# Scan of a hybrid decoder step: one 128-column moving operand for the products on a and r

## What is computed

```python
def wkv7_step(S, inp):
    r, d, k, v, a, b = inp
    sa = jnp.einsum('bhij,bhj->bhi', S, a)
    S = S * d[:, :, None, :] + sa[..., None] * b[:, :, None, :] + v[..., None] * k[:, :, None, :]
    return S, jnp.einsum('bhij,bhj->bhi', S, r)
...
    S_new, o = lax.scan(wkv7_step, S0.astype(f32), seq)
```

## Time and profile before

| | |
|---|---|
| median of 3 runs | 2534.65 us (2529.38 to 2535.4) |
| profiled execution, its own time | 2534.88 us |
| its span in the trace | 2532.9 us |
| mean granted clock of TensorE | 0.967 |
| TensorE busy | 2401.2 us, 95% of the span |
| VectorE, ScalarE, GpSimd busy | 44%, 15%, 21% |
| the eight iterations of the scan | 1266.6 to 1486.1 us |

### The profile page before, as it was taken

How to read it: one execution, slowest core, us unless ns; L and a number is a source line. 1 busy time by engine, 2 the same in 40 slices (tenths; PEclk the granted TensorE clock), 3 DMA queues, 4 the chain that set the end, 5 groups by cost and what they waited for, 6 DMA issues and landing times. The chain is left out here.

```text
span 2532.9 us, 51980 instructions
## 1 busy us (share of the span) xinstructions
PE 2401.2 (95%) x22210; PEld 2277.4 (90%) x22210; DVE 1117.5 (44%) x2477; ACT 387.7 (15%) x879; POOL 526.4 (21%) x270
## 2 busy tenths in 40 slices
PE   5999999999999899999788889989999999999996
PEld 4999999999999899888377775979999999999995
DVE  4533434333344454343666663137333444443336
ACT  4100000000000223344611132031000000000003
POOL 3312122121121131111511034123211212212200
PEclk8999999999999999999799997989999999999997
DMA  9223221111111221011310012122111111111102
GB/s 328 84 100 100 69 80 50 50 50 33 50 28 38 87 79 55 26 34 39 117 25 5 5 32 86 42 100 84 51 33 50 28 38 50 50 50 50 33 0 79
DMA packets 160616, 151.19 MB, mean 60 GB/s; under 512 B 21472, under 2 KB 141969, under 8 KB 160072
## 3 DMA queue, kind: packets, MB, share of 16 engines
q1 hardware_dynamic: 159944, 146.75, 18.3%
q10 hardware_dynamic: 144, 2.23, 0.2%
q0 software_dynamic: 384, 0.07, 0.0%
HBM read 137.98 MB, written 11.34 MB: 59 GB/s over the span
## 5 line engine op out<-in xcount | busy, mean ns | idle before, releaser
L475 PE MATMUL bank<-hh,f_up_hi 128*128 128x364 f32 (+1 forms) x2112 | 697.1, 330 | 9.4 <-ACT hh L415 9.4
L477 PE MATMUL bank<-hh,f_up_lo 128*128 128x364 f32 (+1 forms) x2112 | 695.1, 329 | 0.0
L476 PE MATMUL bank<-hl,f_up_hi 128*128 128x364 f32 (+1 forms) x2112 | 695.0, 329 | 0.0
L928 DVE TENSOR_TENSOR f_prod<-f_silu,bank 128x364 f32<-128x364 f32 x132 | 70.2, 532 | 779.7 <-PE bank L477 779.7
L475 PEld LDWEIGHTS bank<-hh,f_up_hi 128*128 128x128 f32 x2112 | 398.1, 188 | 15.8 <-issue 15.4
L490 DVE SCALAR_TENSOR_TENSOR x<-bank,mods,x 128x364 f32<-128x364 f32 (+2 forms) x552 | 310.4, 572 | 201.4 <-PE bank L477 184.4
L476 PEld LDWEIGHTS bank<-hl,f_up_hi 128*128 128x128 f32 x2112 | 398.2, 189 | 0.0
L477 PEld LDWEIGHTS bank<-hh,f_up_lo 128*128 128x128 f32 x2112 | 398.0, 188 | 0.0
L762 POOL TENSOR_TENSOR f_up_lo<-f_up_raw,f_up_hi 128x2048 fp32r<-128x2048 f32 x44 | 202.9, 4612 | 818.4 <-DVE f_up_hi L915 818.4
L475 PE MATMUL bank<-f_a_hi,f_dn_hi 128*128 128x364 f32 (+1 forms) x1056 | 347.4, 329 | 0.0
L477 PE MATMUL bank<-f_a_hi,f_dn_lo 128*128 128x364 f32 (+1 forms) x1056 | 346.9, 328 | 0.0
(11 more groups left out here) (380 smaller groups left out, 2854.4 us busy)
## 6 DMA issues: line engine op xcount, KB each, us to landing
f_up_raw<-in_ffn_w_gu SPq DMA_DIRECT2D x88, 512.0 KB, 5.0
f_dn_raw<-in_ffn_w_down SPq DMA_DIRECT2D x22, 1024.0 KB, 7.6
ada<-in_w_ada SPq DMA_DIRECT2D x12, 1024.0 KB, 16.1
late<-in_w_ada SPq DMA_DIRECT2D x12, 1024.0 KB, 4.8
w_in_raw<-in_w_in SPq DMA_DIRECT2D x16, 512.0 KB
gates<-in_w_ada SPq DMA_DIRECT2D x8, 1024.0 KB, 7.0
x_in<-in_x_prompt SPq DMA_DIRECT2D x8, 512.0 KB, 8.8
gate<-in_w_ada SPq DMA_DIRECT2D x4, 1024.0 KB, 11.2
```

The lines of the kernel that those rows point to most:

```text
L475: pe.matmul(out, wh, rh, start=(n == 0), stop=False)
L476: pe.matmul(out, wh, rl, start=False, stop=False)
L477: ins = pe.matmul(out, wl, rh, start=False, stop=(n == last))
L928: dve.tensor_tensor(prod[u % 2][:, 0:n], silu[u % 2][:, 0:n], k.psum[2 * (u % 2) + 1][:, 0:n], ALU.mult).then_inc(up_free, 1)
```

## The change

`aa` and `u` are parts of one tensor `au`. It begins at the address that `aa` had, and `u` begins at the address that it had, so no byte moves. With that one access pattern can reach 64 tokens of a and the same 64 tokens of r. `grams` then makes one matmul with 128 moving columns (a's 64, r's 64) where it made two with 64 columns each, with the same weights. The results go to the same places in the same banks. Waits and semaphores are as they were.

```diff
@@ -196,7 +196,8 @@
-        self.u = self.at("u", U_AT, [P, UC, T])
+        self.au = self.at("au", R1_AT + 2 * PAIRS * TB, [P, 10 + UC, T])
+        self.aa, self.u = self.au[:, 0:PAIRS], self.au[:, 10:]
@@ -1630,7 +1631,6 @@
-    k.aa = k.at("aa", R1_AT + 2 * PAIRS * TB, [P, PAIRS, T])
@@ -1991,6 +1991,8 @@
+    a_and_r = k.au[:, 0:20].rearrange("p (g m) n -> p g m n", g=2)
+
@@ -2126,14 +2128,13 @@
                 b, kk = b_of(c), k_of(c)
+                ar = a_and_r[:, :, 0:PAIRS, HD * c:HD * c + HD].rearrange("p g m j -> p m g j")
+                out_b, out_k = (bank[:].rearrange("p (g m j) -> p m g j", g=2, m=PAIRS) for bank in st.bank)
                 if c == SAMPLE_CHUNK:
-                    heads_mm(pe, half(st.bank[0], 0), b, a_of(c))
-                    heads_mm(pe, half(st.bank[0], 1), b, r_of(c)).then_inc(st.pe, 1)
-                    heads_mm(pe, half(st.bank[1], 0), kk, a_of(c))
-                    heads_mm(pe, half(st.bank[1], 1), kk, r_of(c)).then_inc(st.pe, 1)
+                    heads_mm(pe, out_b, b, ar).then_inc(st.pe, 1)
+                    heads_mm(pe, out_k, kk, ar).then_inc(st.pe, 1)
                     return
-                heads_both(pe, (half(st.bank[0], 0), b, a_of(c), True, True), (half(st.bank[1], 0), kk, a_of(c), True, None))
-                heads_both(pe, (half(st.bank[0], 1), b, r_of(c), True, True), (half(st.bank[1], 1), kk, r_of(c), True, st.pe)).then_inc(st.pe, 1)
+                heads_both(pe, (out_b, b, ar, True, True), (out_k, kk, ar, True, st.pe)).then_inc(st.pe, 1)
```

## The result

The changed kernel takes 2512.04 us (median of 4 runs, 2511.05 to 2512.47), the kernel before 2532.02 us (4 runs, 2527.93 to 2535.4): a ratio of 0.9921, 95% interval 0.9903 to 0.9939. It is 20 us faster, where 13.7 us was forecast, and lies 3 us under the stated range. Later, against 15 runs of the kernel before, the same changed kernel had a ratio of 0.9939 (0.9926 to 0.9953): 2516.09 against 2532.16 us, 16.1 us.

A forecast was written before the change was run, and what follows sets the result against it. The prediction took the scan to be bound by TensorE's code arriving at one 256-instruction block per 3.78 us. Seven iterations' 13.2 us plus 0.5 us for the first, other terms 0, gave 2534.65 - 13.7 = 2521 us, range 2515 to 2529.

The forecast's parts named there:

- What bounds the scan: Scan: TensorE's code arrives in blocks of 256 instructions, one every 3.78 us at best, and TensorE runs dry.
- Records removed: Scan, second to eighth iteration: 128 records fewer each, 7.5 to 7.0 blocks, 1.89 us each, 13.2 us in all.
- Stalls left: Scan iterations: of 4.5 us of stall each, 2.6 us stays, so code still bounds them.
- Array time: Grams: eight 128-column passes at 110 ns, 0.88 us a chunk against 0.93; taken as 0, ends -0.9 and +2 us.
- First iteration: Scan's first iteration: loses the same 128 records, between 0 and 1.9 us; 0.5 us taken.
- the waits for `mk` and for `t`: Scan: TensorE's waits for VectorE's masks and the steps behind them would not take the stalls' place; 0 taken.
- Sample chunk and VectorE: Sample chunk's 64 fewer records: 0 taken, 0.9 us possible. VectorE's waits replacing stalls: 0; as a rival bound, 2528 us, chance 0.10.
- The sum: Whole kernel: 13.2 + 0.5 = 13.7 us off the median of 2534.65 us gives 2521 us, 0.54% less.
- The slower rival: Second FFN behind the scan: moved code makes its loop fetch each pass, up to 34 us lost, 2555 us; chance 0.04.

The follow-up runs named there:

- sample_old: The changed kernel with the old form of the grams in the sample chunk only: 2515.84 us, ratio 0.9936 to the kernel before.
- sample_only: The kernel before with the new form of the grams in the sample chunk only: 2530.02 us, ratio 0.9994 to the kernel before.
- the half dose: The changed kernel with the old grams in odd chunks, 128-column grams only in even chunks and the sample chunk: 2520.49 us, ratio 0.997 to the kernel before.

## Why the prediction missed

**What bounds the scan: right.** The rate of code was read from the earlier trace rows and holds within some per cent in every run. The rule of the Trainium skill ("Runtime: NRT & Kernel Launch", "Instruction fetch mechanics") that crossing a block is mostly hidden doesn't hold here: TensorE stands still for up to 2.0 us at a time, and taking away 64 records a chunk that had no array time of their own gave 12.8 us. Its size of a block does.

**Records removed: the sum is right, the iterations are not.** Seven iterations were to give 13.2 us; they went from 196.9 us (219.48 - 22.57) to 183.2 us (204.37 - 21.13): 13.7 us. Stalls left were to be 2.6 us an iteration, and are 2.4 us in the later five; the iteration 26.5 us, and it is 26.2 us on the mean (183.2 / 7). But each was to give 1.89 us. The second gave 0.4 us (26.51 to 26.13 us, and 26.52 to 26.13 us in the other executions of the two kernels), the six behind it 2.2 us each (2.1 us in the other pair). That the sum came out is in part luck. The second iteration was the fastest before, 13.8 ns a record, and had less stall to give; why it kept most of it isn't shown.

**Array time: right.** A 128-column pass takes 0.11 us and hides as forecast.

**First iteration: mis-sized.** 0.5 us was taken and 1.4 us came (22.57 to 21.13 us). The earlier trace rows shows only two of its three stalls behind "issue"; the same view has one more in front of straight matmuls:

```profile
PEld bank L1920 <- issue: 1.1, 1, 1.1
```

Together they are 3.5 us, near the 4.5 us of a later iteration, so that it was short of code too. After the change they are 1.5 us, and 0.4 to 0.5 us more is spent on each of the waits for `mk` and for `t`, which the prediction had put at nothing. With this the scan was off by 1 us or so: 13.7 us forecast, 15.1 us in the profiled pair, 14.7 us between the means of two executions each (218.3 and 203.6 us from mask to mask).

**Sample chunk and VectorE: right.** 0 was taken for both. `sample_old` and `sample_only` show no gain of the sample chunk; the wait for the state is unchanged, and behind the first iteration no wait for `mk` or `t` shows among the waits of the weight loads.

**The sum: here it failed.** "2534.65 - 13.7 = 2521" sets the scan's gain against three runs and takes all that lies outside the scan as the same in every run, a term of 0; and the range 2515 to 2529 has no room for its spread. The two profiled executions differ by 7.6 us outside the scan. The change in the sixteen chunks isn't needed for that: the kernel before with only the sample chunk new has 2307.0 us outside its scan (2524.3 - 217.3), the changed kernel 2306.0 and 2306.2 us in its two profiles, the kernel before 2313.6 and 2315.5 us. They go with how much of an execution the clock spends at its lower level: 144, 144, 148, 168 and 168 us in that order. The first of these has the scan of the kernel before, and the short clock pieces of the changed one. Both sides of the comparison spread by this: the kernel before had 2520.8 to 2538.3 us in 19 runs beside the half dose, the changed one 2511.3 to 2521.8 us in five. The median of four changed runs, 2512.04 us, was at the low end of that, and the three runs shown of the kernel before were at the high end. The prediction saw runs 5 us below the median and didn't widen the range by them; with that the range would have held. The kernel before, too, came out 2.6 us under the median that the sum starts from (2532.02 us). Against more runs the gap is 16.1 us, of which the scan's 14.7 us is the main part.

**The slower rival** (the second FFN fetching code in its loop) didn't come: behind the scan nothing got longer.

The mean clock of every run is on record, and it bears on the rest of the gap. Within one kernel, a run that spends 1 us more at the lower level takes 0.28 us longer (a straight line through all runs, each set of runs from its own mean; the correlation is 0.73). The 47 runs of the kernel before in the three later comparisons have a mean clock of 0.9691, 156 us at the lower level; the nine of the changed one have 0.9699, 151 us. These 5 us are worth 1.4 us, and 14.7 + 1.4 is the gap of 16.1 us. Whether the change shifts the clock's pieces at all isn't settled: 0.0008 is 1.6 times its own standard error. What makes one execution spend more time at the lower level than another was not varied and stays open. The gain of the scan alone, 14 to 15 us, stands apart from it.

## What to carry to other kernels

Where TensorE has unrolled code of many short fp32 matmuls, look at the distance in records between idle times that the profile puts down to "issue". If it is 256 again and again, and the packets of the instruction queue come at one steady pace, the time of such a stretch is the number of records by some 14.7 ns (each one added or removed moved it by 10 to 14 ns), and merging matmuls, or dropping ones whose array time is hidden, pays even where the share of busy time is high; small matmuls put into a place that doesn't stall cost the same. And when two profiles are compared for an effect below one per cent, take the time of the changed stretch, and see first how far the unchanged ones differ.

## What the runs showed that was not expected

- The arrival of code limits even stretches that show no stall: sixteen matmuls of 4 columns a chunk among the straight ones cost 11 to 15 us in 16 chunks, as much as at the grams, and more than the 8.2 us that their passes take (0.51 us a chunk).
- A pass of 4 columns takes as long as one of 64: 64 ns among the straight matmuls, where one of 64 columns takes 58 ns.
- 64 x 64 quarters with 128 moving columns in two runs of 64, some 43 KB apart in a partition, keep the pace of a plain 128-column pass: 0.11 us with all four quarters at work, 272 ns a record.
- Kernels that are alike outside the scan spend 144 to 168 us of an execution at the lower clock, and their time outside the scan differs by up to 9.5 us with that (2306.0 to 2315.5 us).
